# Attention scores of a chunk as one product with 288 columns, with the two parts and the mask added by DVE

## What is computed

```python
qc = q[:, N_META:].reshape(b, n_chunks, CHUNK, N_KV_HEADS, GQA_GROUP, HEAD_DIM)   # CHUNK = 64
# keys of a chunk: 16 meta tokens, the chunk before, the chunk itself = 144 keys
s = jnp.einsum('bcqhgd,bckhd->bchgqk', q, k) * (HEAD_DIM ** -0.5)
s = jnp.where(mask[None, :, None, None, None, :], s, NEG_INF)     # only the first chunk has masked keys
p = jax.nn.softmax(jnp.concatenate([s, sink], axis=-1), axis=-1)[..., :-1]
o = jnp.einsum('bchgqk,bckhd->bcqhgd', p, v)
```

## Time and profile before

| what | value |
| --- | --- |
| time, median of 3 runs | 1204.64 us (1204.12 to 1990.5) |
| time of the profiled execution | 1205.57 us |
| its span in the trace | 1203.2 us |
| PE busy with products | 1187.1 us (99%) |
| DVE busy | 836.0 us (69%) |
| ACT busy | 625.3 us (52%) |
| POOL busy | 117.8 us (10%) |
| granted clock of PE | 1.00 |

### The profile page before, as it was taken

The page is one execution under the profiler, slowest core; times in us unless marked ns, Lnnn a source line. Parts: engine busy times, 40 slices in busy tenths (PEclk is TensorE's granted clock), DMA queues, the critical chain, the costliest instruction groups (busy, mean ns, idle before and its releaser), DMA issues.

```text
span 1203.2 us, 17461 instructions
## 1 busy us (share of the span) xinstructions
PE 1187.1 (99%) x6026; PEld 1007.5 (84%) x6026; DVE 836.0 (69%) x1464; ACT 625.3 (52%) x1472; POOL 117.8 (10%) x133
## 2 busy tenths in 40 slices
PE   7999999999999999999999999999999999999998
PEld 7887898898898988787888888888878888888887
DVE  4677767667586676568677586675786987756676
ACT  5735356465564665644565564663754444444442
POOL 0000011011050220000011030220310000100001
PEclk9999999999999999999999999999999999999999
DMA  7354329455477323354348354293236544553443
GB/s 232 95 158 155 90 88 221 129 179 170 143 159 191 114 72 123 91 171 159 94 106 203 89 172 135 79 221 95 78 95 218 185 141 140 175 176 125 141 151 133
DMA packets 85486, 171.27 MB, mean 142 GB/s; under 512 B 8464, under 2 KB 11792, under 8 KB 85264
## 3 DMA queue, kind: packets, MB, share of 16 engines
q1 hardware_dynamic: 72288, 129.36, 35.0%
q0 software_dynamic: 13120, 40.90, 14.0%
HBM read 157.64 MB, written 46.14 MB: 169 GB/s over the span
## 4 chain that ended last, share of the span: by engine, by line
PE 78%; DVE 12%; ACT 7%; issue 2%; DMA 0%; ACTq 0%; SPq 0%; DVEq 0%
PE R L1355 12%; PE R L1360 12%; PE R L1356 12%; PE R L1644 3%; PE R L1643 3%; PE R L1642 3%; ACT pm L602 3%; PE OP L1644 2%; PE S L1644 2%; PE OP L1643 2%; PE S L1643 2%; PE OP L1642 2%; PE S L1642 2%; DVE wl L922 2%; DVE pm L922 2%
## 5 line engine op out<-in xcount | busy, mean ns | idle before, releaser
L602 ACT ACTIVATE wh<-raw 128x512 fp32r<-128x512 f32 x384 | 239.5, 629 | 341.3 <-PE OP L1644 164.3
L922 DVE TENSOR_TENSOR wl<-raw,wh 128x512 fp32r<-128x512 f32 x384 | 269.4, 704 | 203.7 <-ACT wh L602 203.4
L1355 PE MATMUL R<-act_h,wh 128*128 128x512 f32 (+2 forms) x1056 | 384.4, 369 | 0.0
L1356 PE MATMUL R<-act_l,wh 128*128 128x512 f32 (+2 forms) x1056 | 378.1, 364 | 0.0
L1360 PE MATMUL R<-act_h,wl 128*128 128x512 f32 (+2 forms) x1056 | 364.6, 365 | 0.0
L1356 PEld LDWEIGHTS R<-act_l,wh 128*128 128x128 f32 x1056 | 198.9, 188 | 29.2
L1355 PEld LDWEIGHTS R<-act_h,wh 128*128 128x128 f32 x1056 | 198.4, 188 | 29.3 <-issue 0.3
L1360 PEld LDWEIGHTS R<-act_h,wl 128*128 128x128 f32 x1056 | 189.3, 188 | 32.4
L602 ACT ACTIVATE pm<-OP 16x128 fp32r<-16x128 f32 x256 | 68.3, 267 | 5.5
L1642 PE MATMUL R<-wh,mix_h 128*128 128x512 f32 x168 | 65.4, 389 | 0.0
L1643 PE MATMUL R<-wl,mix_h 128*128 128x512 f32 x168 | 65.4, 389 | 0.0
(11 more groups left out here) (246 smaller groups left out, 2003.9 us busy)
## 6 DMA issues: line engine op xcount, KB each, us to landing
raw<-w_in_blocks SPq DMA_DIRECT2D x272, 256.0 KB, 2.7
wsum<-w_out_in POOLq DMA_DIRECT2D x24, 1024.0 KB, 11.5
raw<-wsum SPq DMA_DIRECT2D x64, 256.0 KB, 2.7
raw<-w_out_in SPq DMA_DIRECT2D x48, 256.0 KB, 3.2
c<-xcat SPq DMA_DIRECT2D x32, 256.0 KB, 3.6
out<-c POOLq DMA_DIRECT2D x28, 256.0 KB, 2.9
mixed<-xcat SPq DMA_DIRECT2D x10, 512.0 KB, 4.7
mx<-mixed SPq DMA_DIRECT2D x8, 512.0 KB, 3.5
```

Source lines behind the costliest of these rows:

```text
L602: return nc.scalar.activation(dst, src, ACT.Copy)
L922: return nc.vector.tensor_tensor(dst, a, b, ALU.subtract)
L1355: mm(o, wh[:, b, w], xh, start=(k == 0), stop=False)
L1356: mm(o, wh[:, b, w], xl, start=False, stop=False)
```

## The change

The keys' two parts are put side by side in one tensor `band`, and `band_h` and `band_x` are views of it. PE makes one product with 288 columns (144 with the high part, 144 with the low part) for a chunk. One bank of `S` now holds one chunk, so a unit goes in two parts of two chunks: part 0 after block 4u+3, part 1 after block 4u+4. DVE adds the two halves of each row into `prob` (`score_sums`, a TENSOR_REDUCE over pairs whose members lie 144 columns apart), for part 0 at slot 4u+4 and part 1 at slot 4u+5. Part 1 of the products waits until part 0 was added, since it uses the same banks. The product that added the mask is gone; there DVE adds the mask, and the sums take three instructions. `row_max` reads `prob` on SBUF and moves to slot 4u+5, `exps` reads and writes `prob` and moves to slot 4u+6, and `normalise` moves to slot 4u+7.

```diff
+        band = sbi("band", [P, 2, KVH, (NCH + 1) * BAND], f32r)
+        band_h, band_x = band[:, 0, :, :], band[:, 1, :, :]
...
                             nc.scalar.activation(
-                                prob[:, c, :], S[:, c // 2, (c % 2) * KEYS:(c % 2 + 1) * KEYS], ACT.Exp,
+                                prob[:, c, :], prob[:, c, :], ACT.Exp,
                                 bias=nmax[:, c:c + 1], accum_out=den[:, c:c + 1]).then_inc(s_ex, 1)
...
-                        todo[4 * u + 5].append((exps, u))
+                        todo[4 * u + 6].append((exps, u))
...
+                    def score_sums(u, part):
+
+                        dve.wait_ge(s_s, ONE + 2 * (G * UNITS + u) + part + 1)
+                        if G + u:
+                            dve.wait_ge(s_pn, G * UNITS + u)
+                        to = prob[:, 2 * part:2 * part + 2, :]
+                        both = S[:, :, 0:2 * KEYS].rearrange("p b (s k) -> p b k s", s=2)
+                        if h == 0 and u % 2 == 0 and part == 0:
+                            nc.vector.tensor_reduce(to[:, 0, CHUNK:KEYS], both[:, 0, CHUNK:KEYS, :], AX.X, ALU.add)
+                            nc.vector.tensor_tensor(to[:, 0, 0:CHUNK], S[:, 0, 0:CHUNK],
+                                                    cst[:, C_MASK:C_MASK + CHUNK], ALU.add)
+                            nc.vector.tensor_reduce(to[:, 1, :], both[:, 1, :, :], AX.X, ALU.add).then_inc(s_sm, 1)
+                        else:
+                            nc.vector.tensor_reduce(to, both, AX.X, ALU.add).then_inc(s_sm, 1)
+
                     def row_max(u):
-                        dve.wait_ge(s_s, ONE + G * UNITS + u + 1)
-                        nc.vector.tensor_reduce(
-                            smax[:, :].rearrange("p (b c) -> p b c", b=2),
-                            S[:, :, 0:2 * KEYS].rearrange("p b (c k) -> p b c k", c=2),
-                            AX.X, ALU.max).then_inc(s_mx, 1)
+                        dve.wait_ge(s_sm, ONE + 2 * (G * UNITS + u + 1))
+                        nc.vector.tensor_reduce(smax[:, :], prob, AX.X, ALU.max).then_inc(s_mx, 1)
...
                     for u in range(UNITS):
+                        todo[4 * u + 4].append((score_sums, u, 0))
+                        todo[4 * u + 5].append((score_sums, u, 1))
+                        todo[4 * u + 5].append((row_max, u))
                         todo[4 * u + 1].append((qdiag, u))
-                        todo[4 * u + 4].append((row_max, u))
-                        todo[4 * u + 6].append((normalise, u))
+                        todo[4 * u + 7].append((normalise, u))
...
-                    def scores(u):
-                        pe.wait_ge(s_qdl, G * UNITS + u + 1)
-                        pe.wait_ge(s_ex, ONE + (G * UNITS + u) * (QUAD + 1))
-                        pe.wait_ge(s_kbh, 8 * (h + 1))
-                        pe.wait_ge(s_kbl, ONE + h + 1)
-                        for c in range(QUAD):
+                    def scores(u, part):
+                        n = G * UNITS + u
+                        if part == 0:
+                            pe.wait_ge(s_qdl, n + 1)
+                            pe.wait_ge(s_kbh, 8 * (h + 1))
+                            pe.wait_ge(s_kbl, ONE + h + 1)
+                        pe.wait_ge(s_sm, ONE + 2 * n + part)
+                        for c in (2 * part, 2 * part + 1):
                             ch = (u % 2) * QUAD + c
-                            o = S[:, c // 2, (c % 2) * KEYS:(c % 2 + 1) * KEYS]
                             at = slice(ch * BAND, ch * BAND + KEYS)
-                            q = qs[:, c, :, :].rearrange("p a t -> p (a t)")
-                            masked = h == 0 and ch == 0
-                            mm(o, q, band_h[:, e, at], start=True, stop=False)
-                            last = mm(o, q, band_x[:, e, at], start=False, stop=not masked)
...
+                            last = mm(S[:, c % 2, 0:2 * KEYS].rearrange("p (s k) -> p s k", s=2),
+                                      qs[:, c, :, :].rearrange("p a t -> p (a t)"), band[:, :, e, at],
+                                      start=True, stop=True)
                         last.then_inc(s_s, 1)
...
-                        when.setdefault(4 * u + 3, []).append((scores, u))
+                        for part in range(2):
+                            when.setdefault(4 * u + 3 + part, []).append((scores, u, part))
```

More of the change, by code:

```diff
@@ L120, in sbi @@
             return inner.enter_context(nc.sbuf_tensor(name, shape, dt))
-        band_h = sbi("band_h", [P, KVH, (NCH + 1) * BAND], f32r)
-        band_x = sbi("band_x", [P, KVH, (NCH + 1) * BAND], f32r)
+        band = sbi("band", [P, 2, KVH, (NCH + 1) * BAND], f32r)
+        band_h, band_x = band[:, 0, :, :], band[:, 1, :, :]
         v_s = sbi("v_s", [P, NCH, 2, HD], f32r)
@@ L288, in hymba_layer @@
         s_s = sem("s_s")
+        s_sm = sem("s_sm")
         s_mx = sem("s_mx")
@@ L347, in hymba_layer @@
         from_one = [s_me, s_wl, s_pwl, s_d, s_blk, s_kbl, s_o, s_s, s_oe, s_dl, s_mix, s_tp,
-                    s_ex, s_pl, s_pve, s_pvr, *s_gv, *s_gt]
+                    s_ex, s_sm, s_pl, s_pve, s_pvr, *s_gv, *s_gt]
         block = ctx.enter_context(nc.Block())
@@ L777, in mix_high @@
                     if n < 2:
-                        act.wait_ge(s_s, ONE + OUT_UNITS)
+                        act.wait_ge(s_s, ONE + 2 * OUT_UNITS)
                     elif n < 4:
@@ L797, in qdiag @@
                     def qdiag(u):
-                        act.wait_ge(s_s, ONE + G * UNITS + u)
+                        act.wait_ge(s_s, ONE + 2 * (G * UNITS + u))
                         q = mixed[:, bass.ds(PAIRS + g * 2 + u // 2, 1),
@@ L1384, in first_group @@
                     if k == 0:
-                        pe.wait_ge(s_ex, ONE + GROUPS * UNITS * (QUAD + 1))
+                        pe.wait_ge(s_sm, ONE + 2 * GROUPS * UNITS)
                     elif k == 2:
@@ L1499, in group @@
                     G = h * GROUPS + g
-                    def scores(u):
-                        pe.wait_ge(s_qdl, G * UNITS + u + 1)
-                        pe.wait_ge(s_ex, ONE + (G * UNITS + u) * (QUAD + 1))
-                        pe.wait_ge(s_kbh, 8 * (h + 1))
-                        pe.wait_ge(s_kbl, ONE + h + 1)
-                        for c in range(QUAD):
+                    def scores(u, part):
[6 more added lines that the diff above has]
+                        for c in (2 * part, 2 * part + 1):
                             ch = (u % 2) * QUAD + c
-                            o = S[:, c // 2, (c % 2) * KEYS:(c % 2 + 1) * KEYS]
                             at = slice(ch * BAND, ch * BAND + KEYS)
-                            q = qs[:, c, :, :].rearrange("p a t -> p (a t)")
-                            masked = h == 0 and ch == 0
-                            mm(o, q, band_h[:, e, at], start=True, stop=False)
-                            last = mm(o, q, band_x[:, e, at], start=False, stop=not masked)
-                            if masked:
-                                last = mm(o, ident, cst[:, C_MASK:C_MASK + KEYS],
-                                          start=False, stop=True)
+                            last = mm(S[:, c % 2, 0:2 * KEYS].rearrange("p (s k) -> p s k", s=2),
+                                      qs[:, c, :, :].rearrange("p a t -> p (a t)"), band[:, :, e, at],
+                                      start=True, stop=True)
                         last.then_inc(s_s, 1)
@@ L1563, in events @@
                     def events(s):
-                        for f, u in when.get(s, ()):
-                            f(u)
+                        for f, *a in when.get(s, ()):
+                            f(*a)
                     n0 = KV_BLKS + Q_BLKS + g * G_BLKS
@@ L1614, in _ @@
                     pe.wait_ge(s_gv[2], ONE + HALVES * GROUPS)
-                    pe.wait_ge(s_ex, ONE + OUT_UNITS * (QUAD + 1))
+                    pe.wait_ge(s_sm, ONE + 2 * OUT_UNITS)
                 elif n == HK:
```

## The result

The changed kernel takes 1255.62 us (median of 4 runs, 1255.06 to 1256.02), the kernel before on the same chip 1204.38 us. The ratio is 1.0427, with a 95% interval from 1.0414 to 1.0440: slower by 51.2 us. The forecast was 1250.5 us, 5.1 us less than measured. One execution of the kernel before took 1990.5 us and one of the experiment `sum_first` 3044.23 us; the ratios leave these two slow ones out.

What follows compares the result with a forecast made beforehand. PE's own work was taken as the bound, busy 99% of the span. 1205.6 - 13 (saving) + 28 (collision) + 32 (other waits) = 1252.6 us, less 2 for returned slack: 1250.5 us, forecast range 1236 to 1258.

Steps and rivals of the forecast that it cites:

- PE's saving: Score products on PE: 32 units save 0.35 us each and 8 masks 0.24 us each, 13 us in all.
- The sums: DVE's two sums per unit: 0.67 us of queue each, 1.0 us with the mask; a reduction itself takes 0.75 us.
- Part 1 of unit 2: PE's scores after unit 1's transposes wait for DVE's first sum: 1.0 us in the first half, 0.7 in the second.
- The collision: DVE's two-SBUF-input instructions in `normalise` wait for POOL, about 1.0 us each, delaying unit 1's transposes; 28 us on PE.
- The sign I named: Trace sign of POOL's collision: PE's longest waits for `pnm` grow by about 1 us from group to group.
- The other waits: PE's waits apart from POOL's collision: 3.7 us per first-half group and 4.3 per second-half group, 32 us.
- first sum of unit 3: PE waits for DVE's chain from unit 1's transposes to this sum: 0.6 us, 1.4 in the second half.
- transposes, all but unit 1's: The same chain on DVE and ACT again makes unit 3's transposes on PE wait 0.65 us per group.
- `values` of the last unit: At a group's end PE waits 1.8 us for `p_low`, of which 0.3 us is paid already.
- the clock: Rival: PE's waits lower its clock to 1.2 GHz for one block in 4 groups, 11 us; 0.13 shared with slow sums.
- the chances: 0.55 forecast, 0.13 clock or slow sums, 0.18 harmless POOL collision; 0.78 for a time above 1228.7 us.
- My layout of the chain: Unit 1 of group 1, first half: `normalise` ends at 257.0 instead of 254.47, using up 4.1 us of slack before the transposes.

Runs made afterwards that it cites:

- sum_first: The changed kernel with only the second sum, the maximum and `nmax` moved ahead of `p_low`; 1210.40 us, ratio 1.0050 to the kernel before.
- after_one_add: The changed kernel with POOL making one addition per pooling tile instead of g+1; 1242.14 us, ratio 1.0317 to the kernel before.
- both_first: The changed kernel with the second sum and maximum ahead of `p_low` and `normalise` ahead of `o_out`; 1201.53 us, ratio 0.9977 to the kernel before.
- before_moved: The kernel before with only the places of `row_max`, `exps` and `normalise` moved as in the change, without sums; 1241.24 us, ratio 1.0309.
- before_load: The kernel before with two unused DVE reductions of 512 elements per unit, at slots 4u+7 and 4u+8; 1222.67 us, ratio 1.0147.
- norm_first: The changed kernel with only `normalise` moved ahead of `o_out`; 1243.37 us, ratio 1.0326 to the kernel before.

## Why the prediction was right, and where its terms were off

**PE's saving** was put at 13 us. It is 32 x (0.91 - 0.53) + 8 x 0.24 = 14 us. The products of 288 columns are 0.13 us apart, as read off the line between 272 and 512 columns.

**The sums** were put at 0.75 us, and a sum takes 0.753. With the mask I had taken 1.0 us for the three instructions; they hold DVE for 0.73 us. Part 1 of unit 2 waits 0.56 us in two groups of the first half, 0.29 in the third and not at all in the fourth, where 1.0 was forecast, and 0.50 in three of the second instead of 0.7; the 0.27 us of the sums is a part of the difference in the first half.

**The collision** was the right mechanism, shown by `after_one_add`, and the term that was mis-sized: 28 us forecast, and unit 1's transposes wait 16.1 us. The sign I named, growth of about 1 us from group to group, is there (0.7 to 1.0 us). In group 1 POOL met three instructions, as many as I had taken, but held them for 1.9 us and not 3: the step that failed is the price of 1.0 us for each, worked out from the 1.3 us between POOL's instructions, where they lose 0.5 to 1.1 us by how they fall against POOL's. In group 3 five are held, for 4.0 us, not 5. And I had left `normalise` no slack, while the waits of PE ahead of it, the missed one above all, gave some back: the transposes wait 0.3 us less than `o_out` and `normalise` lose in group 1, and 0.5 less in group 3.

The Trainium skill, "SBUF — State Buffer", section "Who interferes with whom", which the prediction had drawn on, puts the exclusive lock on instructions of DVE with two inputs from SBUF beside POOL's reads, and leaves TENSOR_REDUCE out. The trace agrees: 10 of the sums lie beside POOL's multiplications and additions by over half their length, and all 56 keep to 743 to 758 ns. In `both_first` maxima lie beside POOL's additions too, and take 0.75 us.

**The other waits** were put at 32 us. Over the 8 groups, in us:

| wait | forecast | measured |
| --- | --- | --- |
| part 1 of unit 2 | 4 x 1.0 + 4 x 0.7 = 6.8 | 2.9 |
| first sum of unit 3 | 4 x 0.6 + 4 x 1.4 = 8.0 | 5.1 |
| transposes, all but unit 1's | 8 x 0.65 = 5.2 | 6.3 |
| `values` of the last unit | 8 x 1.8 = 14.4 | 12.0 |

That is 26.3 us instead of 34.4, of which 2.4 was paid before. The last unit's `values` wait 1.54 to 1.58 us in seven groups and 1.06 in one. The first sum of unit 3 waits 0.83 to 1.17 us in five groups, and not at all in three: these three stand behind the waits of 2.24 to 3.50 us, in which DVE could catch up (behind the fourth such wait, of 3.27, it still waits 0.83).

**What the sum lacked.** First, the wait for `pv_out`, 7.9 us. The step that failed is the one on what PE saves: I counted it as pure gain. Before, 0.9 us of scores (1.15 with the mask) stood between PE's last product of the first pooling tile and its first of the second, and ACT's copy ran in that time, with nothing ahead of it. Now the scores there are a part of 0.26 us, and `exps`, a slot later, are in ACT's way. `before_moved`, where `exps` come a slot later too but the scores there are whole, has no such wait at all. `both_first`, whose maximum comes in time for `exps`, still waits 0.54 to 0.60 us there in each group: that is the lost cover; in the second half of the changed kernel the wait is 1.25 to 1.40, and the difference is ACT's being late. Second, each restart: PE's waits as shown don't contain all of what a wait costs. In the timeline above the second of two score products begins about 0.13 us behind 257.05, so a product without a wait would begin at about 257.3; it begins at 258.13, 0.82 us later, and the idle shown is 0.65. About 0.16 us for each of 44 waits, where there were 8 before, makes 6 us more. Third, the clock, which I had held as a rival with 11 us: the chip did lower it.

**The account.** 1203.2 (span before) - 14 (saving) + 50.3 - 2.4 (waits) + 6 (restarts) + up to 8.6 (clock, below) = 1251.7, and the span is 1252.7 us. That it closes to 1 us is partly luck, since the last two terms are rough, and idle time inside a slow stretch is counted both as a wait and in the clock. The forecast of 1250.5 came close because a collision too large by 12 us and other waits too large by 8 stood against some 22 us of missing terms (7.9, 6 and 8.6); that they nearly cancel is luck. The direction and the size of the slowdown were right; three of its parts were not. In the chances, 0.55, 0.13 and half of 0.18 add up to 0.77 and not 0.78, which changes nothing.

**Order and load.** My layout of the chain took both together and did not say which is the cause. The runs divide it: the places alone make 37 us (`before_moved`), the rest of the change another 14 net of PE's saving, and with the two places corrected all 51 are gone (1201.53 us).

## What to carry to other kernels

When work moves from a full engine to one with much free time, ask where in that engine's queue it stands and what it pushes back, before asking how much it is. A link of a chain that is put behind an unrelated long step (here the maximum behind `p_low`) makes what waits for it late on the other engines too; the same work ahead of that step cost 45 us less, and 54 with `normalise` moved as well. And what is removed from the bound engine may have been the cover of someone else's copy, so look at which wait stands right behind it.

## What the runs showed of the hardware

The granted clock fell behind short waits of a PE that is otherwise full. In the changed kernel PE waits 3.50 us for `pnm`:

```profile
434.79 1.11 PE L1538 MATMUL PT<-cst,scr 128*128 128x128 f32 x4 [3.50 <-DVE pnm L1132]
```

The windows after it, a row for each 4 us; the first number behind POOL's is the granted clock:

```profile
432.00:436.00 4.00, 1.21 (x5) 0.93 (x5) 4.00 (x8) 0.02 (x1) 2.50 (x3) 0.72 0.00 0
436.00:440.00 4.00, 4.00 (x18) 3.88 (x18) 1.65 (x5) 3.61 (x12) 0.00 (x0) 0.50 0.49 135
440.00:444.00 4.00, 4.00 (x33) 4.00 (x32) 3.79 (x9) 2.15 (x9) 0.00 (x0) 0.93 0.00 0
```

0.50 is the 1.2 GHz level: between 436 and 440 us PE is busy all the time and gets 18 products done, where 33 fit into the next window. That is some 3 us lost for a wait of 3.5. The same shows behind the waits of 2.47, 2.24 and 3.27 us in groups 2 and 3 (lowest windows 0.57, 0.57 and 0.67), not behind those of 1.58 us and less. Summed over the windows below 1.00, one less the clock makes 8.6 us. The Trainium skill, "TensorE: Matmul & The Clock Gate", section "HAM oscillation — how this bites in real kernels", has the clock fall behind a gap in PE's work; this kernel shows it for gaps as short as 2.24 us though its PE is busy for 95% of the span, and `before_load`, with PE busy for 98%, for single ones of 1.71 and 1.73 us (windows of 0.78 and 0.73):

```profile
660.77 0.76 PE L1547 MATMUL OP<-pt,v_s 128*128 128x256 f32 x4 [1.71 <-DVE pm L924]
```

It did not fall there behind one of 1.70 us, nor in `before_moved` behind those of 2.22 and 2.28 us, while it did behind 2.29. In `sum_first` it fell behind waits of 1.22 and 2.01 us, each with another of 0.50 a microsecond later (windows of 0.63 and 0.58), but not behind an equal pair of 2.01 and 0.50 in the group between them; in `norm_first` it fell at pairs of 1.3 and 1.2 us, two microseconds apart (0.74 and 0.66), while `after_one_add`, with waits of at most 1.6 us, kept 1.00. So the length of one wait doesn't decide it alone; what does is left open.

A small instruction of DVE with two inputs of SBUF can be held as long as a large one: `dtot`, 4 results per partition, took 1.02 us beside POOL instead of 0.15.
